# RWKV recurrence: v centred as it is turned, roots written for 64 channels, the crossed block from the masked products, the bonus as two products of a split r k

## The chip, the cores and the metric

The kernel runs on 1 core of one Trainium2 chip. The metric is the device time of one execution in microseconds (us). Three runs of the kernel before gave 2329.27 to 2331.78, with a median of 2330.76.

## The reference, cut to what matters

A two-layer network over 512 tokens of 1024 channels: FFN, an attention mixer, FFN, then a mixer of RWKV-7 heads and chunked attention, an MLP, a convolution and an MLP. The change lies in the RWKV part (8 heads of 64 channels):

```python
    a = jax.nn.sigmoid(a0 + xa @ a2)
    g = jax.nn.sigmoid(xg) @ g2
    kk = heads(k * k_k)
    kk = kk / jnp.maximum(jnp.sqrt(jnp.sum(kk * kk, axis=-1, keepdims=True)), 1e-12)
    k = k * (1 + (a - 1) * k_a)
    y = rwkv7_scan(rh, heads(decay), kh, vh, kk, ah)   # S = S*w - (S kk)(kk a)^T + v k^T ; y = S r
    mean = jnp.mean(y, axis=-1, keepdims=True)
    var = jnp.mean(jnp.square(y - mean), axis=-1, keepdims=True)
    y = (y - mean) * lax.rsqrt(var + GN_EPS)
    y = y * lnx_w + lnx_b
    bonus = jnp.sum(rh * kh * r_k, axis=-1, keepdims=True) * vh
    y = (y + bonus) * g
```

The channel of y is the channel of v, and y is linear in v. So a v whose mean over the head's 64 channels is taken off gives y less its mean.

## The kernel before

All large products are "split": a weight unit (128 rows by 8 blocks of 128, 512 KB) is loaded by SP, its high part is made by ACT (`stream_high`, L101) and its low part by POOL (`stream_low`, L114), and the tensor engine (PE) runs three fp32r products of 512 columns for each block (`split_products`, L133 to L135: high x high, high weight x low, low weight x high). Four slots hold units in a ring. A unit's products may start once its low part is there (`c.s_lo`).

The recurrence works on 4 pairs of heads (`PAIRS`), each pair on all 128 partitions (64 channels a head) and 8 chunks of 64 tokens. For pair j, PE runs `prod` (L1998), `lab` (L2005, and the crossed products L2008), four `turn`s by transposes (L2019: V, B, K, A), five levels of `w` (L2029), `d` (L2049), `e` (L2053), which invert the chunk's triangular matrix, with `lv` (L2036) in level 0, then `u`, `z` (L2060, L2064), `ru`, `g` (L2072, L2076), `yl`, `h` (L2082 to L2090), seven sequential steps `s2` to `s7` (L2100) and `y` (L2115).

The order on each engine is written out by hand, and PE runs its queue in order. Between the steps of pair j stand:

- `fill(j, slot)`: products of pair j+2's input weights, in single blocks (the table `FILL`), so that PE has work while DVE or ACT finish what the next step needs. For pair 3 these belong to the attention that follows.
- `prepare(j+1, part)`: the next pair's inputs. PE: `lora_w`, `lora_a`, `kknorm` (squares summed for a head into 2 columns), `kkb` (L1818: the reciprocal norm spread over 64 channels by `by_channel_pe`), `bonus` (L1939). ACT: shifts k, r, v; `sq`; `root`; `sigw`, `siga`, `ld`, `rks`; the exponentials. DVE: `raw`, `rec`, `L` (a scan), `kk`, `bon`. POOL: `k`, `kk0`, `r`, `v`, `ka`, `kfin`, `rk`, `lp`, `le`, three low parts, then `A`, `b0`, `B`, `K`, `Bp`, `Kp`, `pend`, `R` (L2400 to L2410).
- `tail(j-1, name)`: the previous pair's normalisation. `mean` (L1950: head sums of y, one fp32 product of 512 columns), `yc` (DVE, L2561: y less the mean), `ysq` (ACT), `var` (L1956), `yroot` (ACT), `yrec` (DVE), `yrb` (L1818: spread over channels), `yn`, `ysum` (DVE), `gate` (L1965), `out`.

Each engine counts its steps with a semaphore per list (`PREPARATION`, `STEPS`, `TAIL`); `PL(j, "R")` means "wait for POOL's step R of pair j", `PA`, `PV`, `PE_` the same for ACT, DVE and PE, `TA`, `TV`, `TE` for tails, `V`, `A`, `E` for the steps. Pair 0's preparation runs ahead of the loop, and there `prepare(0, "bonus")` stands on PE right before pair 0's `prod`:

```python
    prepare(0, "kkb")
    unit_part(1, KU + 4, 3 * KU)
    prepare(0, "bonus")
    for j in range(PAIRS):
        q, t = j + 1, j - 1
        if j == 0:
            PL(j, "K")
```

In the loop, `tail(t, "gate")` and `prepare(q, "bonus")` stand behind `h`, ahead of `s2`. On PE `unit_part` waits at a unit's first block for its low part; the second unit of a pair's fill begins at slot 7, behind level 4's `e`.

Of the kernel before, what the change touches and what calls it, by code (L numbers as in the profile page):

```python
# [2169 lines left out]
def rwkv_act(act, c, w, base, m, a, passes):  # L2170
# [15 lines left out]
    def prepare(j, part):  # L2186
# [23 lines left out]
        elif part == "root":  # L2210
            PE_(j, "kknorm")
            prepared("root", act.activation(w.norm[:, 0], ps[:, b_norm, 0:2 * TT].rearrange("p (b s) -> p b s", s=2),
                                            ACT.Sqrt))
# [9 lines left out]
        else:  # L2223
# [9 lines left out]
            prepared("ePe", act.activation(w.ePe, w.ePe, ACT.Exp))  # L2233

    def tail(t, name):
        if t < 0:
            return
        if name == "ysq":
            TV(t, "yc")
            ended("ysq", act.activation(w.ysq, w.yc, ACT.Square))  # L2240
        else:
            TE(t, "var")
            norms = ps[:, tail_banks(base, t)[2], 8:8 + 2 * TT]
            ended("yroot", act.activation(w.ynorm[:, 0], norms.rearrange("p (b s) -> p b s", s=2), ACT.Sqrt,
                                          bias=c.gn_eps[:, 0:1], scale=1.0 / HD))
# [1389 lines left out]
```

## Time and profile before

| | |
|---|---|
| median of three runs | 2330.76 us |
| the profiled execution | 2329.62 us, its span 2327.9 us |
| mean granted clock of PE | 0.993 |
| PE, DVE, ACT, POOL busy | 2289.9 (98%), 1156.0 (50%), 914.2 (39%), 1163.3 (50%) |
| prod of pairs 0 to 3 starts at | 1145.21, 1193.98, 1246.81, 1299.59 us |

Times in rows are from the span's start. A timeline row has the start, the time from the start of the first of its instructions to the end of the last, engine, line, operation, what is written from what, and the count; in brackets is the idle time of the engine before it and what ended it. PE's products overlap: the price of a step is from its start to the start of the next. An fp32 product of 512 columns shows as two records, a transposed block of 128 columns as one.

### The profile page before, as it was taken

The numbers are of one execution on the slowest core, as the hardware profiler recorded it, in microseconds if no ns is written. First come the engines' busy times: TensorE is split into PE (matmuls) and PEld (weight loads), VectorE is DVE, ScalarE is ACT, GpSimd is POOL, SyncE is SP. The second block draws the span as 40 slices with busy tenths as digits, with TensorE's granted clock in tenths as the row PEclk, the third lists the DMA queues.
The fourth block names the chain that finished last, engine by engine and source line by source line (L and its number), as shares of the span: only waits on it lengthen the run. The fifth ranks groups of instructions, "written<-read, shape, count | busy, mean of one in ns | idle before, by whom it ended". The sixth has DMA issues, their size and how long they took to land.

```text
span 2327.9 us, 37006 instructions
## 1 busy us (share of the span) xinstructions
PE 2289.9 (98%) x13984; PEld 1892.3 (81%) x13984; DVE 1156.0 (50%) x1772; ACT 914.2 (39%) x1456; POOL 1163.3 (50%) x687
## 2 busy tenths in 40 slices
PE   8999999999999999999999999999999999999998
PEld 7888887888888888878777778888888878888887
DVE  5442146267744331367554466614626986731732
ACT  5332225467753321255654264222234435222222
POOL 5444444545565554444555444444445973544442
PEclk9999999999999999999999999999999989999999
DMA  4332333320033333331101113332332332333331
GB/s 167 99 97 93 99 99 103 123 65 2 1 101 99 99 99 92 97 126 57 54 30 41 59 51 100 99 99 91 99 99 75 99 100 82 99 99 93 96 97 57
DMA packets 56127, 200.11 MB, mean 86 GB/s; under 512 B 6224, under 2 KB 6480, under 8 KB 56016
## 3 DMA queue, kind: packets, MB, share of 16 engines
q1 hardware_dynamic: 54432, 195.82, 26.5%
q10 hardware_dynamic: 1584, 2.75, 0.4%
q8 instruction: 77, 1.26, 0.2%
q14 instruction: 34, 0.28, 0.0%
HBM read 196.45 MB, written 2.10 MB: 85 GB/s over the span
## 4 chain that ended last, share of the span: by engine, by line
PE 50%; DVE 2%; ACT 1%; POOL 1%; issue 0%; DVEq 0%; ACTq 0%
PE ps L133 15%; PE ps L134 15%; PE ps L135 14%; PE ps L642 1%; DVE ps L3096 0%; PE ps L2053 0%; PE ps L657 0%; POOL sb_w_lo L114 0%; PE ps L2049 0%; PE ps L2100 0%; PE ps L2029 0%; PE ps L1998 0%; PE ps L2019 0%; DVE sb_ak_lo L1015 0%; DVE sb_L L2544 0%
## 5 line engine op out<-in xcount | busy, mean ns | idle before, releaser
L114 POOL TENSOR_TENSOR sb_w_lo<-sb_w_raw,sb_w_hi 128x1024 fp32r<-128x1024 f32 (+1 forms) x361 | 886.2, 2458 | 931.5 <-ACT sb_w_hi L101 930.0
L133 PE MATMUL ps<-sb_xn_hi,sb_w_hi 128*128 128x512 f32 x1688 | 670.3, 397 | 5.9 <-DVE sb_xn_lo L175 3.1
L134 PE MATMUL ps<-sb_xn_lo,sb_w_hi 128*128 128x512 f32 x1688 | 658.4, 390 | 0.0
L135 PE MATMUL ps<-sb_xn_hi,sb_w_lo 128*128 128x512 f32 x1688 | 658.2, 390 | 0.0
L101 ACT ACTIVATE sb_w_hi<-sb_w_raw 128x1024 fp32r<-128x1024 f32 x362 | 379.7, 1055 | 483.8 <-PE ps L135 457.6
L133 PEld LDWEIGHTS ps<-sb_xn_hi,sb_w_hi 128*128 128x128 f32 x1688 | 316.8, 188 | 78.3 <-issue 4.0
L135 PEld LDWEIGHTS ps<-sb_xn_hi,sb_w_lo 128*128 128x128 f32 x1688 | 317.0, 188 | 67.7
L134 PEld LDWEIGHTS ps<-sb_xn_lo,sb_w_hi 128*128 128x128 f32 x1688 | 317.1, 188 | 65.6 <-issue 2.2
L133 PE MATMUL ps<-sb_hid_hi,sb_w_hi 128*128 128x512 f32 x864 | 336.3, 389 | 2.0 <-DVE sb_hid_lo L401 2.0
L135 PE MATMUL ps<-sb_hid_hi,sb_w_lo 128*128 128x512 f32 x864 | 336.1, 389 | 0.0
L134 PE MATMUL ps<-sb_hid_lo,sb_w_hi 128*128 128x512 f32 x864 | 336.1, 389 | 0.0
L133 PEld LDWEIGHTS ps<-sb_hid_hi,sb_w_hi 128*128 128x128 f32 x864 | 162.2, 188 | 36.5 <-DVE sb_hid_lo L401 2.8
L135 PEld LDWEIGHTS ps<-sb_hid_hi,sb_w_lo 128*128 128x128 f32 x864 | 162.2, 188 | 33.8
L134 PEld LDWEIGHTS ps<-sb_hid_lo,sb_w_hi 128*128 128x128 f32 x864 | 162.2, 188 | 33.4
L470 DVE SCALAR_TENSOR_TENSOR ps<-ps,sb_rs 128x512 f32<-128x512 f32 x32 | 22.4, 700 | 286.7 <-PE ps L135 286.7
L2808 DVE TENSOR_TENSOR sb_hid_lo<-sb_h,sb_hid_hi 128x512 f32 x64 | 143.6, 2243 | 7.9
L2792 ACT ACTIVATE sb_gate<-ps 128x512 f32<-128x512 f32 x64 | 38.3, 598 | 248.6 <-PE ps L135 248.6
L393 DVE TENSOR_TENSOR sb_h<-sb_gate,ps 128x512 f32<-128x512 f32 x44 | 30.3, 689 | 207.8 <-PE ps L135 206.2
L401 DVE TENSOR_TENSOR sb_hid_lo<-sb_h,sb_hid_hi 128x512 f32 x44 | 115.8, 2632 | 5.4
L378 ACT ACTIVATE sb_gate<-ps 128x512 f32<-128x512 f32 x44 | 26.4, 600 | 199.6 <-DVE ps L389 199.6
L448 ACT ACTIVATE ps<-ps 128x512 f32<-128x512 f32 x56 | 32.8, 585 | 168.3 <-DVE ps L505 127.6
L502 DVE SCALAR_TENSOR_TENSOR ps<-ps,sb_rs 128x512 f32<-128x512 f32 x32 | 22.4, 700 | 130.5 <-PE ps L135 130.5
(487 smaller groups left out, 2987.4 us busy)
## 6 DMA issues: line engine op xcount, KB each, us to landing
sb_w_raw<-weights SPq DMA_DIRECT2D x365, 512.0 KB, 3.5
sb_stage<-x SPq DMA_DIRECT2D x4, 512.0 KB, 4.8
out<-sb_out_stage SPq DMA_DIRECT2D x8, 256.0 KB, 2.9
sb_abias<-table ACTq DMA_DIRECT2D x4, 256.0 KB, 4.8
sb_lora_w<-lora ACTq DMA_DIRECT2D x2, 256.0 KB, 2.8
sb_rstd<-table ACTq DMA_DIRECT2D x1, 256.0 KB, 2.7
sb_root<-table ACTq DMA_DIRECT2D x1, 256.0 KB, 3.0
sb_ss<-table ACTq DMA_DIRECT2D x1, 256.0 KB, 4.3
```

What stands on the lines that cost most here:

```text
L101: act.activation(c.w_hi[:, slot, 0:width], c.w_raw[:, slot, 0:width], ACT.Copy).then_inc(c.s_hi, 1)
L114: pool.tensor_tensor(c.w_lo[:, slot, 0:width], c.w_raw[:, slot, 0:width], c.w_hi[:, slot, 0:width].bitcast(F32), ALU.subtract).then_inc(c. ...
L133: pe.matmul(out, hi, rhs_hi(k0 + k), start=first, stop=False)
L134: pe.matmul(out, hi, rhs_lo(k0 + k), start=False, stop=False)
L135: mm = pe.matmul(out, lo, rhs_hi(k0 + k), start=False, stop=last)
L378: act.activation(c.gate[:, s // 2], c.ps[:, slot], ACT.Silu).then_inc(c.s_act, 1)
L393: dve.tensor_tensor(c.h[:, f], c.gate[:, f], c.ps[:, u % RING], ALU.mult).then_inc(c.s_evac, 2)
L401: dve.tensor_tensor(c.hid_lo[:, i * 2 + f], c.h[:, f], c.hid_hi[:, i * 2 + f].bitcast(F32), ALU.subtract).then_inc(c.s_hid, 1)
L448: act.activation(c.ps[:, 4 + n % 2], new, ACT.Square).then_inc(c.s_sq, 1)
L642: mm = pe.matmul(c.ps[0:p.kind.rows, T_BANK + bank, col + (i - q0) * P:col + (i - q0) * P + P], a.p[n % 3][:, at:at + p.kind.rows], a.diag ...
L2792: act.activation(c.gate[:, s % 2], c.ps[:, slot], ACT.Relu).then_inc(c.s_act, 1)
L2808: dve.tensor_tensor(c.hid_lo[:, i * RING + s], c.h[:, s % 2], c.hid_hi[:, i * RING + s].bitcast(F32), ALU.subtract).then_inc(c.s_hid, 1)
```

## The change

1. The turn of V becomes an fp32 product with `c.centre` (the identity less 1/64 within a head), so tok's v, and with it y, has no mean over a head. `mean` on PE and `yc` on DVE go; `ysq` reads YL and moves ahead of the turns on ACT, `var` from level 1 to level 0, `yrec` to level 1, and `lora_a` no longer waits for `yc`.
2. The reciprocal is taken first on DVE (`kmax`, `rec`; `yadd`, `yrec`), then ACT takes the root of it, written out over 64 channels (512 columns), and PE spreads it by four plain transposes instead of eight fp32 products (`kkb`, `yrb`).
3. The crossed block E[1] comes from M's second half by two DVE operations of 64 partitions; its 8 products in `lab` go.
4. Of the three weights of a pair, two are split on POOL between `v` and `ka` and on ACT between `value` and `root`; the third stays where it was.
5. `bonus` is two fp32r products of a constant with `rk_hi` (ACT, behind the exponentials) and `rk_lo` (POOL, `rkl` behind `Kp`).

```diff
-    pool = ["k", "kk0", "r", "v", "ka", "kfin", "rk", "lp", "le", "A", "b0", "B", "K", "Bp", "Kp", "pend", "R"]
+    pool = ["k", "kk0", "r", "v", "ka", "kfin", "rk", "lp", "le", "A", "b0", "B", "K", "Bp", "Kp", "rkl", "pend", "R"]
...
-def by_channel_pe(pe, c, bank, norm):
-
-    for b in range(TT):
-        for s in range(2):
-            mm = pe.matmul(c.ps[HALF[s], bank, b * P:b * P + P], norm[:, 1, b, s:s + 1].broadcast_to([P, HD]), c.ident[:],
-                           start=True, stop=True)
-    return mm
+def spread(norm):
+    return norm[:, 1].rearrange("p b s -> p (b s)").unsqueeze(2).broadcast_to([P, 2 * TT, HD])
...
         elif part == "lora_a":
-            if j >= 2:
-                TV(j - 2, "yc")
             mm = pe.matmul(ps[:, b_turned], w.lora_w[HD:P, 0, cols], w.lora_in[HD:P, 0], start=True, stop=True)
         elif part == "kkb":
-            PV(j, "rec")
+            PA(j, "root")
             if j >= 2:
-                TA(j - 2, "yroot")
-            mm = by_channel_pe(pe, c, b_norm, w.norm)
+                TV(j - 2, "yrec")
+            for b in range(TT):
+                mm = pe.transpose(ps[:, b_norm, b * P:b * P + P], w.tmp2[:, b * P:b * P + P], c.ident[:])
         else:
-            PL(j, "rk")
             PV(j, "kk")
-            mm = pe.matmul(ps[:, bonus_bank(u, j)], c.ones_head[:], w.rk, start=True, stop=True)
+            bank = ps[:, bonus_bank(u, j)]
+            PA(j, "rkh")
+            pe.matmul(bank, c.ones_part, w.rk_hi[:], start=True, stop=False)
+            PL(j, "rkl")
+            mm = pe.matmul(bank, c.ones_part, w.rk_lo[:], start=False, stop=True)
...
-        if name == "mean":
-            if t < PAIRS - 1:
+        if name == "var":
+            if t == PAIRS - 2:
                 pe.wait_ge(c.s_evac, first_unit(t + 2) + START + 3)
-            mm = pe.matmul(ps[:, bank], c.ones_head[:], w.YL[:], start=True, stop=True)
-        elif name == "var":
-            if t < PAIRS - 2:
-                PA(t + 2, "root")
             TA(t, "ysq")
...
-            TV(t, "yrec")
-            mm = by_channel_pe(pe, c, bank, w.ynorm)
+            TA(t, "yroot")
+            for b in range(TT):
+                mm = pe.transpose(ps[:, bank, b * P:b * P + P], w.ysq[:, b], c.ident[:])
...
         done("prod", mm)
-        tail(t, "mean")
         fill(j, 0)
...
-        for b, p in ((b, p) for b in range(TT) for p in range(2)):
-            mm = pe.matmul(ps[across(1, p), 5, TT * CH + b * CH:TT * CH + b * CH + CH], w.BK[HALF[1], 2 * b + p, 0],
-                           AR[HALF[1], 0, token(b, p)], start=True, stop=True)
...
-                mm = pe.transpose(ps[:, bank, b * P:b * P + P], sources[x][:, b * P:b * P + P], c.ident[:])
+                turned = ps[:, bank, b * P:b * P + P]
+                if name == "V":
+                    mm = pe.matmul(turned, w.v[:, b * P:b * P + P], c.centre, start=True, stop=True)
+                else:
+                    mm = pe.transpose(turned, sources[x][:, b * P:b * P + P], c.ident[:])
...
             fill(j, 2 + lv)
-            if lv == 1:
+            if lv == 0:
                 tail(t, "var")
...
-    V(t, "y")
-    tail(t, "mean")
     out_early(4, 6)
...
         elif part == "root":
-            PE_(j, "kknorm")
-            prepared("root", act.activation(w.norm[:, 0], ps[:, b_norm, 0:2 * TT].rearrange("p (b s) -> p b s", s=2),
-                                            ACT.Sqrt))
+            PV(j, "rec")
+            prepared("root", act.activation(w.tmp2.rearrange("p (x n) -> p x n", n=HD), spread(w.norm), ACT.Sqrt))
...
+            PL(j, "rk")
+            if j >= 1:
+                PE_(j - 1, "bonus")
+            prepared("rkh", act.activation(w.rk_hi[:], w.rk, ACT.Copy))
...
         if name == "ysq":
-            TV(t, "yc")
-            ended("ysq", act.activation(w.ysq, w.yc, ACT.Square))
+            V(t, "y")
+            ended("ysq", act.activation(w.RU[:], w.YL[:], ACT.Square))
...
+        tail(j - 1, "ysq")
         for name, x, bank in TURNS:
...
-        tail(j - 1, "ysq")
         prepare(j + 1, "value")
+        if j < PAIRS - 1:
+            for u in range(base + 6 + 3 * j, base + 8 + 3 * j):
+                high(u)
...
         if j < PAIRS - 1:
-            for u in range(base + 6 + 3 * j, base + 9 + 3 * j):
-                high(u)
+            high(base + 8 + 3 * j)
...
         shifted(j, 2, "v", w.v)
+        if j >= 1:
+            stream_low(pool, c, base + 6 + 3 * j, base + 8 + 3 * j)
         PA(j, "siga")
...
         if j >= 1:
-            stream_low(pool, c, base + 6 + 3 * j, base + 9 + 3 * j)
+            stream_low(pool, c, base + 8 + 3 * j, base + 9 + 3 * j)
...
         prepared("Kp", pool.tensor_tensor(w.BKp[:, 1], w.k[:], w.ePe, ALU.mult))
+        PA(j, "rkh")
+        prepared("rkl", pool.tensor_tensor(w.rk_lo[:], w.rk, w.rk_hi[:].bitcast(F32), ALU.subtract))
...
-            ended("yc", dve.scalar_tensor_tensor(out=w.yc, in0=blocks(ps[:, bank]), scalar=-1.0 / HD, in1=blocks(w.YL[:]),
-                                                 op0=ALU.mult, op1=ALU.add))
...
+            sums = ps[:, norms, 8:8 + 2 * TT].rearrange("p (b s) -> p b s", s=2)
+            ended("yadd", dve.tensor_scalar(w.ynorm[:, 0], sums, 1.0 / HD, GN_EPS, ALU.mult, ALU.add))
+            ours(t, "yadd")
...
+        own(j, "mm1")
+        dve.tensor_tensor(w.E[HALF[1], 1], w.M[HALF[0], 1, :, 0], first[HALF[0]], ALU.mult)
+        done("em1", dve.tensor_tensor(w.E[HALF[0], 1], w.M[HALF[1], 1, :, 0], first[HALF[1]], ALU.mult))
         E(j, "lab")
-        done("em1", dve.tensor_tensor(w.E[:, 1], ps[:, 5, TT * CH:].rearrange("p (b n) -> p b n", n=CH), first, ALU.mult))
...
-            elif lv == 2:
+            elif lv == 1:
                 prepare(q, "rec")
+                tail(t, "yrec")
...
+        pool.tensor_scalar(c.centre, c.ones_head[:], -1.0 / HD, None, ALU.mult).then_inc(c.s_zeroed, 1)
...
+        pool.tensor_tensor(c.centre, c.centre, c.ident[:], ALU.add).then_inc(c.s_zeroed, 1)
...
+        pool.tensor_tensor(c.ones_part, c.ones_head[:], c.ones_head[:], ALU.mult).then_inc(c.s_zeroed, 1)
```

## Rows read from the trace of the kernel before

**Rows 1.** The page's first part, and the waits of 1145 to 1352 us.

```profile
PE 2289.9 (98%) x13984; PEld 1892.3 (81%) x13984; DVE 1156.0 (50%) x1772; ACT 914.2 (39%) x1456; POOL 1163.3 (50%) x687
...
PE ps L133 <- POOL sb_w_lo L114: 2.9, 3, 1.1
```

**Rows 2.** PE's timeline, pair 1 from prod to level 0.

```profile
1193.98 1.98 PE L1998 MATMUL ps<-sb_AR,sb_BK 64*64 64x128 f32 x64
1195.89 1.12 PE L1950 MATMUL ps<-sb_rYL,sb_ones_head 128*128 128x512 f32 x2
...
1198.33 0.69 PE L2005 MATMUL ps<-sb_BK,sb_AR 64*64 64x64 f32 x32
1198.86 0.63 PE L2008 MATMUL ps<-sb_AR,sb_BK 64*64 64x64 f32 x16
1199.42 0.50 PE L133 MATMUL ps<-sb_xn_hi,sb_w_hi 128*128 128x512 f32 x1
...
1200.22 0.60 PE L2019 MATMUL ps<-sb_ident,sb_rkv 128*128 128x128 f32 x4
...
1202.06 0.69 PE L1921 MATMUL ps<-sb_lora_in,sb_lora_w 64*128 64x512 f32 x1
...
1203.61 0.58 PE L2029 MATMUL ps<-sb_D,sb_M 64*64 64x64 f32 x24
```

**Rows 3.** The same timeline, at kkb and at the bonus of pair 1.

```profile
1216.13 1.09 PE L1818 MATMUL ps<-sb_ident,sb_rwkv_norm 128*64 128x128 f32 x16
1217.16 0.50 PE L133 MATMUL ps<-sb_xn_hi,sb_w_hi 128*128 128x512 f32 x1
...
1232.95 1.02 PE L1939 MATMUL ps<-sb_y,sb_ones_head 128*128 128x512 f32 x2
1233.90 0.33 PE L2100 MATMUL ps<-sb_dist,sb_rG 64*64 64x64 f32 x4
```

**Rows 4.** DVE's timeline, levels 2 and 3 of pair 1.

```profile
1214.77 0.69 DVE L2657 TENSOR_TENSOR sb_D<-sb_D,ps 128x512 f32<-128x512 f32 x1 [0.51 <-PE ps L2049]
...
1216.88 1.75 DVE L2544 TENSOR_TENSOR_SCAN sb_L<-sb_dist_local,sb_ss 128x512 f32<-128x512 bf16 x1
```

**Rows 5.** ACT's timeline in pair 1, behind v2.

```profile
1208.48 1.28 ACT L2212 ACT_TABLE_LOAD   x1
...
1212.67 0.69 ACT L2216 ACTIVATE sb_ss<-ps,sb_par 128x512 f32<-128x512 f32 x1
...
1214.96 2.95 ACT L101 ACTIVATE sb_w_hi<-sb_w_raw 128x1024 fp32r<-128x1024 f32 x3
```

**Rows 6.** POOL's timeline in pair 1, from ka to pend.

```profile
1214.04 0.77 POOL L2385 TENSOR_SCALAR sb_y<-sb_root,sb_par,sb_omka 128x512 f32<-128x512 f32 x1 [4.42 <-ACT sb_root L2218]
...
1218.70 1.27 POOL L2393 TENSOR_TENSOR sb_raw<-sb_L,sb_ss 128x512 f32<-128x512 f32 x1 [1.16 <-DVE sb_L L2544]
...
1220.94 7.00 POOL L114 TENSOR_TENSOR sb_w_lo<-sb_w_raw,sb_w_hi 128x1024 fp32r<-128x1024 f32 x3
1227.89 1.09 POOL L2400 TENSOR_TENSOR sb_AR<-sb_rstd,sb_raw 128x512 f32<-128x512 f32 x1
...
1235.28 0.19 POOL L2407 COPY sb_pend<-sb_eP 128x8 f32<-128x8 f32 x1
```

**Rows 7.** PE's timeline, the last record of pair 0's s2.

```profile
1181.13 0.27 PE L2100 MATMUL ps<-sb_dist,sb_rG 64*64 64x64 f32 x1 [0.54 <-issue]
```

**Rows 8.** Ahead of pair 0: POOL's kfin and pend, PE's first prod.

```profile
1131.90 2.08 POOL L2387 TENSOR_TENSOR sb_rkk<-sb_rkk,sb_y 128x512 f32<-128x512 f32 x1
...
1146.83 0.19 POOL L2407 COPY sb_pend<-sb_eP 128x8 f32<-128x8 f32 x1
...
1145.21 1.98 PE L1998 MATMUL ps<-sb_AR,sb_BK 64*64 64x128 f32 x64
```

**Rows 9.** PE behind its longest idle of this stage; the windows view (busy us by engine, PEclk).

```profile
1068.25 0.39 PE L628 MATMUL ps<-sb_ak_hi,sb_aq 128*128 128x256 f32 x1 [3.09 <-DVE sb_aq L1011]
...
1070.00:1072.00 2.00, 1.27 (x5) 0.86 (x5) 1.97 (x8) 1.51 (x3) 1.90 (x1) 0.50 0.00 0
```

More of the change, by code:

```diff
@@ L1600, in rwkv_preparation @@
     pe = ["lora_w", "lora_a", "kknorm", "kkb", "bonus"]
-    act = ["k1", "k2", "r1", "r2", "sq", "v1", "v2", "root", "sigw", "siga", "ld", "rks", "eP", "ePi", "ePp", "ePn", "ePe"]
-    dve = ["raw1", "raw0", "raw2", "rootmax", "rec", "L", "kk", "bon"]
-    pool = ["k", "kk0", "r", "v", "ka", "kfin", "rk", "lp", "le", "A", "b0", "B", "K", "Bp", "Kp", "pend", "R"]
+    act = ["k1", "k2", "r1", "r2", "sq", "v1", "v2", "root", "sigw", "siga", "ld", "rks", "eP", "ePi", "ePp", "ePn", "ePe", "rkh"]
+    dve = ["raw1", "raw0", "raw2", "kmax", "rec", "L", "kk", "bon"]
+    pool = ["k", "kk0", "r", "v", "ka", "kfin", "rk", "lp", "le", "A", "b0", "B", "K", "Bp", "Kp", "rkl", "pend", "R"]
     return pe, act, dve, pool
@@ L1623, in rwkv_tail @@
 def rwkv_tail():
-    return ["mean", "var", "yrb", "gate"], ["ysq", "yroot"], ["yc", "yrec", "yn", "ysum", "out"]
+    return ["var", "yrb", "gate"], ["ysq", "yroot"], ["yadd", "yrec", "yn", "ysum", "out"]
 PREPARATION = dict(zip(("pe", "act", "dve", "pool"), rwkv_preparation()))
@@ L2238, in tail @@
         if name == "ysq":
-            TV(t, "yc")
-            ended("ysq", act.activation(w.ysq, w.yc, ACT.Square))
-        else:
[L2242 to L2245, printed above, removed]
+            V(t, "y")
+            ended("ysq", act.activation(w.RU[:], w.YL[:], ACT.Square))
+        else:
+            TV(t, "yrec")
+            ended("yroot", act.activation(w.RU[:].rearrange("p (x n) -> p x n", n=HD), spread(w.ynorm), ACT.Sqrt))
     act.wait_ge(c.s_pe, base + START + 1)
@@ L2537, in prepare @@
         elif part == "rec":
-            PA(j, "root")
-            prepared("rootmax", dve.tensor_scalar(w.norm[:, 0], w.norm[:, 0], 1e-12, None, ALU.max))
-            mine(j, "rootmax")
+            PE_(j, "kknorm")
+            sums = ps[:, b_norm, 0:2 * TT].rearrange("p (b s) -> p b s", s=2)
+            prepared("kmax", dve.tensor_scalar(w.norm[:, 0], sums, 1e-24, None, ALU.max))
+            mine(j, "kmax")
             prepared("rec", dve.reciprocal(w.norm[:, 1], w.norm[:, 0]))
@@ L2556, in tail @@
             return
-        bank, b_gate, _ = tail_banks(base, t)
-        if name == "yc":
-            TE(t, "mean")
-            own(t, "y")
-            ended("yc", dve.scalar_tensor_tensor(out=w.yc, in0=blocks(ps[:, bank]), scalar=-1.0 / HD, in1=blocks(w.YL[:]),
-                                                 op0=ALU.mult, op1=ALU.add))
-        elif name == "yrec":
-            TA(t, "yroot")
+        bank, b_gate, norms = tail_banks(base, t)
+        if name == "yrec":
+            TE(t, "var")
+            sums = ps[:, norms, 8:8 + 2 * TT].rearrange("p (b s) -> p b s", s=2)
+            ended("yadd", dve.tensor_scalar(w.ynorm[:, 0], sums, 1.0 / HD, GN_EPS, ALU.mult, ALU.add))
+            ours(t, "yadd")
             ended("yrec", dve.reciprocal(w.ynorm[:, 1], w.ynorm[:, 0]))
@@ L2567, in tail @@
             TE(t, "yrb")
-            ended("yn", dve.scalar_tensor_tensor(out=w.yc, in0=w.yc, scalar=c.column("l0_lnx_w_2", t),
+            ended("yn", dve.scalar_tensor_tensor(out=w.yc, in0=blocks(w.YL[:]), scalar=c.column("l0_lnx_w_2", t),
                                                  in1=blocks(ps[:, bank]), op0=ALU.mult, op1=ALU.mult))
@@ L2637, in rwkv_dve @@
         done("E", dve.tensor_tensor(Et, Et, over(c.ident_head[:]), ALU.add))
-        tail(t, "yc")
         for lv in range(len(LEVELS)):
@@ L2660, in rwkv_dve @@
             done(f"E{lv}", dve.tensor_tensor(Et, Et, banked(4), ALU.add))
-        tail(t, "yrec")
         tail(t, "yn")
@@ L2694, in rwkv_dve @@
     add_early(0)
-    tail(t, "yc")
     maxima(0)
```

8 lines of the change are left out of this document (added).

## The prediction

> **What bounds the kernel.** I read the page first: the matmul engine (PE) is busy for 98% of the span [rows 1], so only PE's time counts, and another engine counts where PE waits for it. The change lies in the recurrence, about 1107 to 1370 us. The chain of waits there shows one wait of weight: PE for a weight's low part from POOL, 2.9 us in three times [rows 1], once in each of pairs 0 to 2, behind level 4. Then I took PE's timeline by start times, since its durations overlap. A slot of one weight row (three fp32r products of 512 columns) takes 0.80 from start to start [rows 2], 0.23 a product. Pairs 1 and 2 last 52.8 us each, nearly all issue. So the first reading is that less PE work is less time; the second, that PE runs its queue in order, and a wait put in it stops everything behind.
>
> **PE work, per pair.** All prices are starts to next starts.
> - "mean" goes: 512 columns in fp32 are two records, 0.95 as in the bonus (below). But prod ends at 1195.89 and lab at the earliest waits for DVE's first mask. The six fill products take 1.6, the mask is ready about 1.4 after prod's end, so lab can start at 1197.5 where it started at 1198.33 [rows 2]. I take 0.85.
> - The crossed products of lab (16 records) go: 0.56 [rows 2], less 0.1 for the change of tile shape that the rest now pays: 0.47.
> - V turned by a product instead of transposes: the 16 transposes of all four turns take 1.84 [rows 2], 0.46 a turn. No fp32 product of 128 by 128 columns stands in this stage; the bounds are two records for each transpose's one (0.9) and kkb's 16 records (1.03). I take 0.95, what as many columns cost in one 512-column product, so +0.5.
> - lora_a in pairs 1 and 2 waited for "yc": the two lora products took 1.55 [rows 2] where with no wait two 64-row halves run side by side in 1.06 (pair 0, 1152.96 to 1154.02). 0.5 gained.
> - kkb and yrb: 16 records, 1.03 [rows 3], against four transposes, 0.44: 0.58 each. Behind kkb stands the scan of L, 1.75 on DVE [rows 4]: D3 is asked for 0.4 before the scan ends, so of kkb's 0.58 I count 0.2.
> - The wait for the low weight goes: 2.9 idle, and by start times 0.7, 1.2 and 1.2. Next late there is E4 on DVE, which comes about 0.1 before u: covered, barely.
> - var moves one level up, at the same cost; the roots' 0.24 wait ahead of it goes. The reciprocals with their maximum and sum now all stand between W1 and D1 on DVE; ahead of D2, with two of them in place, it still idled 0.51 [rows 4], the price of the two more is 0.4. If they came later, D1 and w2 would, by as much. The second half of E costs DVE 0.35 more (256 columns, half of a 0.69 operation); PE has the turns and loras above it, except in pair 0, where w0 stands right behind E: +0.35 there.
>
> In pair 1: 0.85 + 0.47 - 0.5 + 0.5 + 0.24 + 0.2 + 1.2 + 0.58 = 3.5, so PE reaches the bonus at 1229.4 instead of 1232.95 [rows 3].
>
> **The bonus** is two fp32r products at 0.23, about 0.65 with the changes of shape, 0.3 less than the one in fp32. But its second product waits for rkl, which POOL makes behind A, b0, B, K, Bp, Kp. This is the step that decides, so I follow the chain.
> - ACT, pair 1: v2 ended at 1208.46 (the table load follows at 1208.48); ysq moves ahead (0.5 less), PE's earlier lv takes 1.3 off: 1206.7. Two high parts at 0.98, table load 1.28, both roots now 512 wide at 0.62 (as ACT's other 512-column operations), table load 1.28, sigw 0.59, siga 0.68 [rows 5]: 7.03, so siga ends at 1213.7; before, ka started at 1214.04.
> - POOL: its two low parts now lie in the idle stretch before siga, done by 1212.6. ka, kfin, rk to 1217.3 (3.5), lp and le 2.24, one low part 2.33, A to Kp 7.39 (1227.89 to 1235.28), rkl 1.25 as its like lp [rows 6]. Sum: 1213.8 + 3.5 + 2.24 + 2.33 + 7.39 + 1.25 = 1230.5.
> PE wants it at 1229.6, behind the first product, and waits 0.9. s2 then starts at 1230.9 instead of 1233.90: 3.0 gained in each of pairs 1 and 2.
> - Pair 0: in pair 1 rkl comes 36.5 after prod's start. In pair 0 ACT has no yroot (0.6 less), but lv comes 0.9 later, since DVE makes bon and three raws before the mask, and b0 ran 0.4 shorter: 36.4. PE's bonus stood 33.9 after prod (1179.07); less 0.7 and 0.2, plus 0.35, it would be there at 33.3 and, behind the first product, waits 2.8. The four records of s2 are then through at 37.0; before, the last one started at 1181.13, 35.9 after prod, behind an issue gap of 0.54 that a wait hides [rows 7]: +1.0.
> - Before pair 0: POOL's Kp ends at 1146.83; the longer root adds 0.44, rkl 1.25: 1148.5. PE comes to the bonus at 1143.7 (kkb 0.58 earlier), runs one product, and waits 4.5 us with prod behind, which before only needed K. Prod starts at 1148.9 instead of 1145.21 [rows 8]: +3.7. Nothing covers this; DVE's bon and the next pair's raw come later by as much.
> - Pair 3: mean 0.85, lab 0.47, yrb 0.58, less 0.5 for V and 0.1 for tA: 1.3 gained. The last tail: mean 0.95 and yrb 0.58, of which softmax waits give part back: 1.0 (0 to 1.5).
> Three constants on POOL, the rkh on ACT (0.6, before u is asked for) and the weights high earlier: nothing, POOL and ACT idle there; without that cover rkh would cost 0.6 a pair.
>
> Sum: 3.7 + 1.0 - 3.0 - 3.0 - 1.3 - 1.0 = -3.6 us.
>
> **The clock.** PE idled 3.1 us before 1068.25, and the granted clock fell from 2.4 to 1.2 GHz (0.50 in the stretch after) [rows 9]; products of 512 columns then started 0.43 apart instead of 0.23. Here 4.5 us idle are made ahead of pair 0. I take the fall as happening: bonus and prod are 2.4 slower, the fill loses 0.3, and lab's slack of 0.5 takes some: +2.2 (bounds: 0 with no fall; 3.2 if all work up to lab runs at half speed and no slack helps). Pair 0's wait of 2.8 us at the bonus is just under the one seen; I count no fall there. The Trainium skill (TensorE: Matmul & The Clock Gate, Part 1) says that the throttled clock is the default and that activity releases it, so that an idle gap costs more than its own length. By that rule this change, whose gains are less PE work, gives part of them back, and without it the sum would stay at -3.6; the trace agrees with the rule in the one gap shown.
>
> Result: -3.6 + 2.2 = -1.4. The profiled execution took 2329.62, so 2328.2; the median, 1.14 above it, 2330.76, so **2329.4 us**: no change. A measurement tells about 0.2% here, 4.7 us.
>
> **Rivals.**
> - *PE's work alone decides* (rkl is ready in time, because POOL's chain is shorter than I make it). Then the prelude gives 1.0, pair 0 0.55, pairs 1 and 2 3.9 each, pair 3 1.3, tail 1.0: -11.7, so 2319.1. For it: POOL is idle half the time, and my chain adds ten durations. Against: the order of the queue, which the prelude shows in absolute times. If the chain is only 1.5 us shorter everywhere, the waits ahead of pair 0 and in it give 3.0, those of pairs 1 and 2 1.8, and with the clock's fall -1.4 becomes -6.2: 2324.6. Chance 0.25 for both together.
> - *POOL's chain is longer, and PE's clock falls twice* (slower). Place: from siga to rkl. POOL's kfin took 2.08 in the prelude beside DVE [rows 8], and 1.28 elsewhere (lp 1.27 [rows 6]); two such of ten operations make a pair's chain 1.5 longer. Then three pairs lose 4.5, and pair 0's wait is past 4 us, so the clock falls there too, +2.6: -1.4 + 4.5 + 2.6 = +5.7, 2336.5. It decides from 1.2 us a pair up. The Trainium skill (SBUF, two separate sides) has a rule for it: a DVE operation with two SBUF inputs and a GpSimd operation exclude each other on a shared port pair; the halves of E and the roots' move make a few more of these. The trace has both durations, so it does not speak against it. Chance 0.23.
> - *No fall of the clock*: 2327.2. Chance 0.12.
> - The forecast itself, 0.40.
>
> **Numbers.** Faster by over 0.2% (below 2326.1) 0.25, within 0.2% 0.52, slower 0.23. The range reaches from the shorter chain, less 1.6 for the prices of V, the tail and E, to the slower rival: 2323 to 2337.
>
> **What would show it.** PE: a gap of over 4 us between two products of the bonus ahead of the first prod, ended by POOL; gaps near 3, 1 and 1 us at the same line in pairs 0 to 2; no wait for the low weight behind level 4; clock 0.5 after the first gap. From prod to prod about 49.8 us in pairs 1 and 2 (52.8 before); in pair 0 49.8 (48.8 before), or 52 with the clock's fall. Four records each for kkb and yrb. POOL: two low parts between v and ka. It is wrong if the gap ahead of prod is under 3 us, or if pairs 1 and 2 shrink by less than 2.

## The result: slower by 0.4%

The kernel after takes **2339.93 us** (median of 6 runs, 2337.16 to 2342.99), the kernel before beside it 2330.60 (6 runs, 2329.27 to 2335.48). The ratio is 1.0039 with a 95% interval of 1.0028 to 1.0050. The prediction was 2329.4 in a range of 2323 to 2337 with "no change" as the likeliest: the time lies outside, on the slow side. The profiled execution of the kernel after took 2341.02 us with a span of 2339.3, 11.4 more than the 2327.9 of before. The medians are 9.3 apart: what follows splits up the 11.4 of the two traces.

The page of the kernel after, and its waits between 1140 and 1360 us, against [rows 1]:

```profile
PE 2288.0 (98%) x13832; PEld 1892.9 (81%) x13832; DVE 1157.0 (49%) x1776; ACT 919.8 (39%) x1460; POOL 1175.0 (50%) x694
...
PE ps L1937 <- POOL sb_rk_lo L2406: 13.4, 4, 5.6
```

PE has 152 instructions and 1.9 us of work less, and the wait for the low weight is gone. In its place stands a larger one: the second product of the bonus waits four times for POOL's low part of r k, 13.4 us in all. A gap below is the time from the start of PE's last product to the start of the next one; the bracket in a row is the idle time, which is shorter. The four gaps are 5.97, 3.63, 3.13 and 3.14 us. Here are the first and the third in PE's timeline:

```profile
1143.22 0.40 PE L1935 MATMUL ps<-sb_rk_hi,sb_ones_part 128*128 128x512 f32 x1
1149.19 0.79 PE L1937 MATMUL ps<-sb_rk_lo,sb_ones_part 128*128 128x512 f32 x1 [5.57 <-POOL sb_rk_lo L2406]
1149.92 3.62 PE L1993 MATMUL ps<-sb_AR,sb_BK 64*64 64x128 f32 x64
...
1238.18 0.79 PE L1935 MATMUL ps<-sb_rk_hi,sb_ones_part 128*128 128x512 f32 x1
1241.31 0.51 PE L1937 MATMUL ps<-sb_rk_lo,sb_ones_part 128*128 128x512 f32 x1 [2.34 <-POOL sb_rk_lo L2406]
1241.75 0.33 PE L2095 MATMUL ps<-sb_dist,sb_rG 64*64 64x64 f32 x4
```

In or behind each of them the granted clock falls, and once more in the last tail. The windows view of the kernel after (stretch, length, busy us of PE, PEld, DVE, ACT, POOL, then PEclk, DMA share, GB/s) shows 0.50 to 0.52, 1.2 GHz, behind the first, third and fourth, and in the tail:

```profile
1150.00:1152.00 2.00, 2.00 (x40) 2.00 (x44) 1.98 (x4) 0.59 (x1) 0.00 (x0) 0.50 0.04 8
...
1242.00:1244.00 2.00, 2.00 (x12) 1.13 (x8) 0.22 (x1) 0.00 (x0) 0.62 (x1) 0.52 0.00 0
...
1296.00:1298.00 2.00, 2.00 (x8) 1.12 (x7) 0.22 (x1) 0.00 (x0) 1.34 (x1) 0.50 0.00 0
...
1372.00:1374.00 2.00, 2.00 (x9) 1.90 (x8) 0.48 (x3) 1.66 (x5) 0.26 (x1) 0.50 0.00 0
```

The 64 records of prod take 3.62 in the first fence; at full clock they took 1.98 [rows 2]. From the first product of each pair to that of the next (for pair 3: to y), in us:

| | prod of pair 0 | pair 0 | pair 1 | pair 2 | pair 3 | y to last gate |
|---|---|---|---|---|---|---|
| before | 1145.21 | 48.77 | 52.83 | 52.78 | 49.37 | 11.60 |
| after | 1149.92 | 53.91 | 52.30 | 53.52 | 47.99 | 12.78 |
| after less before | +4.7 | +5.1 | -0.5 | +0.7 | -1.4 | +1.2 |

The columns add up to +9.9 at the last gate. Another 1.5 come in the 6 us behind it, where the clock falls once more; at 1375.70 the kernel after is 11.4 behind the kernel before, and the spans end 11.4 apart. That last place is one that I had not looked for. PE is done with the fill ahead of pair 3's gate at about 1367.2 and starts the gate at 1370.42. The rows of POOL, DVE and ACT there:

```profile
1362.54 2.38 POOL L114 TENSOR_TENSOR sb_w_lo<-sb_w_raw,sb_w_hi 128x1024 fp32r<-128x1024 f32 x1
...
1362.76 2.19 DVE L766 TENSOR_SCALAR sb_t_negmax<-sb_t_maxima 128x4 f32<-128x4 f32 x1
...
1365.29 0.63 ACT L2239 ACTIVATE sb_rRU<-sb_rwkv_ynorm 128x512 f32<-128x512 f32 x1 [2.50 <-DVE sb_rwkv_ynorm L2564]
1365.94 1.28 ACT L705 ACT_TABLE_LOAD   x1
...
1369.56 0.18 DVE L778 RECIPROCAL sb_t_scale<-sb_t_sums 128x4 f32<-128x4 f32 x1 [1.90 <-ACT sb_later_p L705]
1369.65 0.72 DVE L2567 SCALAR_TENSOR_TENSOR sb_rH<-sb_rYL,sb_par,ps 128x512 f32<-128x512 f32 x1
```

Read it upwards: the gate waits for yn (L2567), which stands on DVE behind scale(0) (L778), which waits for softmax(0) on ACT (it starts with the table load), which stands behind yroot (L2239), which waits for yrec on DVE, behind maxima(0). The last step of maxima(0), L766 on 128 by 4 numbers, took 2.19 us; the same line took 0.17 in the next pass (1367.49). In the kernel before it took 0.63, and yroot did not wait for it:

```profile
1355.62 0.63 DVE L766 TENSOR_SCALAR sb_t_negmax<-sb_t_maxima 128x4 f32<-128x4 f32 x1
...
1355.76 0.27 ACT L2244 ACTIVATE sb_rwkv_ynorm<-ps,sb_gn_eps 128x8 f32<-128x8 f32 x1
1356.05 1.28 ACT L705 ACT_TABLE_LOAD   x1
```

The table load starts 7.1 us behind y there and 8.3 behind it in the kernel after (1348.96 to 1356.05, 1357.64 to 1365.94).

### The profile page after: what moved, and what is told of

Its sections match the earlier page's. It is cut to its first block, busy times and chain, and to the rows that moved or that the text cites. A ratio compares the mean times of both kernels' runs of the same rounds, so it can differ in the third digit from the quotient of the medians.

```text
span 2339.3 us, 36715 instructions
## 1 busy us (share of the span) xinstructions
PE 2288.0 (98%) x13832; PEld 1892.9 (81%) x13832; DVE 1157.0 (49%) x1776; ACT 919.8 (39%) x1460; POOL 1175.0 (50%) x694
## 3 DMA queue, kind: packets, MB, share of 16 engines
q10 hardware_dynamic: 1584, 2.75, 0.3%
q8 instruction: 75, 1.23, 0.2%
## 4 chain that ended last, share of the span: by engine, by line
PE 41%; POOL 7%; issue 3%; DVE 2%; ACT 2%; POOLq 0%; DVEq 0%; ACTq 0%
PE ps L133 12%; PE ps L134 12%; PE ps L135 12%; POOL sb_w_lo L114 2%; POOL sb_caway L3052 1%; PE ps L642 1%; DVE ps L3103 0%; PE ps L1993 0%; PE ps L657 0%; POOL sb_cu_lo L3064 0%; POOL sb_y L2388 0%; ACT sb_w_hi L101 0%; POOL sb_cout L3058 0%; PE ps L2095 0%; POOL sb_rkk L2385 0%
## 5 line engine op out<-in xcount | busy, mean ns | idle before, releaser
L2815 DVE TENSOR_TENSOR sb_hid_lo<-sb_h,sb_hid_hi 128x512 f32 x64 | 151.5, 2367 | 7.9
L401 DVE TENSOR_TENSOR sb_hid_lo<-sb_h,sb_hid_hi 128x512 f32 x44 | 115.8, 2633 | 5.4
```

The costliest lines, as they stand in the source:

```text
L401: dve.tensor_tensor(c.hid_lo[:, i * 2 + f], c.h[:, f], c.hid_hi[:, i * 2 + f].bitcast(F32), ALU.subtract).then_inc(c.s_hid, 1)
L2815: dve.tensor_tensor(c.hid_lo[:, i * RING + s], c.h[:, s % 2], c.hid_hi[:, i * RING + s].bitcast(F32), ALU.subtract).then_inc(c.s_hid, 1)
```

## The experiments

Waits below are gaps from start to start; a time is a median, a ratio is against the kernel before run beside it. Starts, gaps and lengths of pairs are from the one profiled execution of each kernel, which can be up to 3.9 us from the median.

### One product again

```diff
+            PL(j, "rk")
...
-            PA(j, "rkh")
-            pe.matmul(bank, c.ones_part, w.rk_hi[:], start=True, stop=False)
-            PL(j, "rkl")
-            mm = pe.matmul(bank, c.ones_part, w.rk_lo[:], start=False, stop=True)
+            mm = pe.matmul(ps[:, bonus_bank(u, j)], c.ones_head[:], w.rk, start=True, stop=True)
```

> The kernel after with the split of the bonus alone undone: one fp32 product of ones_head and r k again, no high part on ACT, no low part on POOL; everything else stays. Theory A (the second product's wait for POOL's low part, and the clock that falls behind it, are the loss): the four gaps of 5.97, 3.63, 3.13 and 3.14 us are gone, the first product of pair 0 starts near 1145.5 (K's end) in place of 1149.9, and the granted clock stays at 1.00 from 1140 to 1360 but for the last tail; prelude -4.4, pair 0 -5, pairs 1 and 2 -4 to -5 each: 2321 to 2326 us. Theory B (the added work of TensorE is the loss: V as fp32 product, two products, more waits behind them): at most the gaps go and come back at the next wait, 2334 or more. Theory C (POOL's chain A to Kp, later by contention, is the loss): only the prelude changes, 2335 to 2337.

Measured: 2323.98 us, ratio 0.9971 (0.9960 to 0.9982); prod of pair 0 at 1145.60, pairs of 48.78, 49.43, 49.42 and 47.95. Theory A holds and its number with it: 16 us under the kernel after, and 0.3% faster than before. What is left of the loss is in the last tail, whose gap of 3.49 and clock of 0.50 are still there.

### The split kept, its low part early

```diff
+        PA(j, "rkh")
+        prepared("rkl", pool.tensor_tensor(w.rk_lo[:], w.rk, w.rk_hi[:].bitcast(F32), ALU.subtract))
         if j >= 1:
             stream_low(pool, c, base + 8 + 3 * j, base + 9 + 3 * j)
         PV(j, "kk")
...
-        PA(j, "rkh")
-        prepared("rkl", pool.tensor_tensor(w.rk_lo[:], w.rk, w.rk_hi[:].bitcast(F32), ALU.subtract))
```

On ACT the high part stands between ePi and ePp.

> The kernel after with the split kept and only moved: ACT makes the high part behind ePi, POOL the low part right behind le and ahead of A. Theory A: the second product waits for nothing in pairs 0 to 2; in the prelude A to K stand about 0.6 to 1.3 us later, so the first product of pair 0 starts at 1146.0 to 1146.8; pairs 0, 1, 2 shrink as without the split and by some 0.2 each more, since the two products take 0.65 and one takes 0.95: 2321 to 2327 us, within 1.5 us of the kernel with one product. Theory B: 2334 or more. Theory C: POOL's chain is longer in every pair (its operations take 2.1 in place of 1.3 us wherever they stand), a new wait takes the place of the old one: 2332 to 2337.

Measured: 2324.30 us, ratio 0.9973 (0.9963 to 0.9983); prod of pair 0 at 1146.30, pairs of 48.77, 49.17, 49.17 and 47.98. Same operations, same engines, another place in POOL's queue, and 15.6 us less. PE at pair 1's bonus, first with one product, then with two:

```profile
1229.95 1.02 PE L1934 MATMUL ps<-sb_y,sb_ones_head 128*128 128x512 f32 x2
1230.90 0.33 PE L2092 MATMUL ps<-sb_dist,sb_rG 64*64 64x64 f32 x4
```

```profile
1229.78 1.13 PE L1960 MATMUL ps<-sb_lora_in,sb_lora_w 128*128 128x512 f32 x2
1230.34 0.80 PE L1935 MATMUL ps<-sb_rk_hi,sb_ones_part 128*128 128x512 f32 x1
1230.97 0.40 PE L1937 MATMUL ps<-sb_rk_lo,sb_ones_part 128*128 128x512 f32 x1
1231.33 0.33 PE L2095 MATMUL ps<-sb_dist,sb_rG 64*64 64x64 f32 x4
```

The two products take 0.99 from start to start and the one takes 0.95. The saving of 0.26 in pairs 1 and 2 (49.43 to 49.17) comes from the gate in front: its two records take 0.56 where they took 0.96 ahead of the fp32 product, and 0.1 of that is lost on the way to the gate. Pair 0 saves nothing. With POOL's low part ahead of A, K is ready 0.7 later for pair 0, which gives all of the 0.5 back. Free of its wait, the split is worth nothing that can be measured.

### Only TensorE's order changed

```diff
                 fill(j, 8 + ch)
+                if ch == 5:
+                    prepared("bonus", bonus_low(q))
```

`bonus_low` is the wait for rkl and the second product, taken out of the bonus of pairs 1 to 3.

> The kernel after with TensorE's order alone changed: in pairs 0 to 2 the second product of the bonus of the next pair stands behind the fill of the fifth chunk's step, four fills later, in place of right behind the first product. POOL and ACT are untouched, and the prelude keeps its wait of 6 us and its low clock. Theory A: no wait in pairs 0 to 2 and no low clock there; pair 0 keeps 1.6 for the clock it inherits from the prelude: 50.4, pairs 1 and 2 49.1 to 49.3 us long: 2327 to 2329.5 us. Rival (TensorE's wait only moves: DVE's bon or the next pair's products find POOL late): pairs 1 and 2 over 51, 2334 or more.

Measured: 2328.64 us, ratio 0.9989 (0.9980 to 0.9998); pairs of 50.00, 49.49, 49.51 and 47.97. POOL is as late as in the kernel after (rkl ends 37.4 behind prod in both); four fills of 0.9 us now stand between the two products, and PE does not wait at the second. The time is inside theory A's range; pairs 1 and 2 are 0.2 above it and pair 0 is 0.4 under. The prelude's gap of 5.97 is still there. So the loss in pairs 0 to 2 was the place at which PE asked, not POOL's work.

### The low part one operation earlier

```diff
         prepared("Bp", pool.tensor_tensor(w.BKp[:, 0], w.tmp, w.ePe, ALU.mult))
+        PA(j, "rkh")
+        prepared("rkl", pool.tensor_tensor(w.rk_lo[:], w.rk, w.rk_hi[:].bitcast(F32), ALU.subtract))
         prepared("Kp", pool.tensor_tensor(w.BKp[:, 1], w.k[:], w.ePe, ALU.mult))
-        PA(j, "rkh")
-        prepared("rkl", pool.tensor_tensor(w.rk_lo[:], w.rk, w.rk_hi[:].bitcast(F32), ALU.subtract))
```

> The kernel after with POOL's low part one operation (1.26 us) earlier, behind Bp and ahead of Kp. The waits are then 4.7 in the prelude, 2.4 in pair 0, 1.9 in pairs 1 and 2 by every theory. If the low clock is what such a wait brings whatever its length, the gain is the waits' own, 4 times 1.26: 2334.5 to 2335.5 us, and the granted clock still falls to 0.50 in each pair. If the clock's fall hangs on the length of the wait, it stays at 1.00 in pairs 1 and 2, perhaps in pair 0, and 1.5 to 1.7 more go with each: 2329.5 to 2332.5.

Measured: 2332.11 us, ratio 1.0005 (0.9995 to 1.0016; one of the 11 executions took 5033.68, the others 2330.09 to 2338.51), 7.8 under the kernel after where the four waits are only 1.23, 1.22, 1.22 and 1.23 shorter. The gaps are 4.74, 2.41, 1.91 and 1.91 us. The windows of this kernel behind the second and third:

```profile
1190.00:1192.00 2.00, 2.00 (x9) 1.13 (x8) 0.22 (x1) 0.00 (x0) 0.00 (x0) 0.50 0.00 0
...
1242.00:1244.00 2.00, 2.00 (x14) 1.29 (x14) 1.04 (x3) 0.00 (x0) 0.00 (x0) 1.00 0.00 0
```

Pair 0 (54.07) still has the fall, pairs 1 and 2 have not, and they are 49.55 and 49.59 long, against 52.30 and 53.52. So a wait shortened by 1.2 gave 2.75 and 3.93: the rest, 1.5 and 2.7, is what the clock took in those two traces. The time is inside the range of a fall that hangs on the wait's length; that length alone does not decide it, as the counts further down show.

### The split alone, on the kernel before

```diff
-            mm = pe.matmul(ps[:, bonus_bank(u, j)], c.ones_head[:], w.rk, start=True, stop=True)
...
+            pe.matmul(bank, c.ones_part, w.rk_hi[:], start=True, stop=False)
+            PL(j, "rkl")
+            mm = pe.matmul(bank, c.ones_part, w.rk_lo[:], start=False, stop=True)
```

> The kernel before with the split of the bonus alone (two products, high part behind ePe on ACT, low part behind Kp on POOL). Theory A: the second product waits 4 to 5 us in the prelude and 2 to 3.5 in pairs 0 to 2, with clock falls behind most of them: +4 in the prelude, +2 to +5 in each of the three pairs: 2341 to 2349 us. Theory B: the split costs what its products and waits of work cost, under 0.5 a pair, and the prelude's 4: 2335 at most. Theory C (POOL is late only because of the weight parts moved ahead of the gates): waits of under 2 in pairs 1 and 2 and no clock fall there, 2336 to 2339.

Measured: 2355.34 us, ratio 1.0108 (1.0093 to 1.0124), above even theory A's range. The gaps are 3.88, 5.71, 4.03 and 4.14, the pairs 56.42, 58.81, 60.21 and 49.35 long. I had the waits of pairs 0 to 2 at 2 to 3.5 and a loss of 2 to 5 in each. In pair 1 a gap of 4.03 came with 6.0 us of loss; the windows show a low clock for most of 6 us behind it:

```profile
1250.00:1252.00 2.00, 2.00 (x8) 1.13 (x8) 0.23 (x3) 0.00 (x0) 0.00 (x0) 0.50 0.00 0
1252.00:1254.00 2.00, 2.00 (x8) 1.14 (x8) 0.83 (x3) 0.00 (x0) 0.00 (x0) 0.50 0.00 0
1254.00:1256.00 2.00, 2.00 (x9) 1.14 (x9) 0.33 (x2) 0.00 (x0) 0.00 (x0) 0.65 0.00 0
```

PE ran 8 records in 2 us, where it ran 14 at full clock in the fence of the experiment before this one. Pair 2 lost 7.4. The other parts of the change thus save 15 us beside the split (2355.34 to 2339.93).

### yn ahead of scale(0) in the last tail

```diff
     maxima(1)
+    tail(t, "yn")
     scale(0)
-    tail(t, "yn")
```

> The kernel after with one line of DVE's last tail moved: yn ahead of scale(0). Theory A (the last tail's 2.75 us are TensorE's wait of 3.26 at the gate, for yn behind scale(0) behind softmax(0), and the clock that falls behind it): yn ends near 1368.4 in place of 1370.37, the wait is 1.2 to 1.4, the clock stays at 1.00 there, and the time is 3.0 to 3.6 lower than the kernel after's, 2336.3 to 2336.9. Rival: scale(0) is then 0.7 later and turned attention waits for it: 0 to 1 lower, 2339 to 2340. No other stage changes in either.

Measured: 2336.72 us, ratio 1.0031 (1.0022 to 1.0040): 3.2 under the kernel after, by one line. PE now waits 1.03 at the gate (a gap of 1.43) and the clock stays at 1.00:

```profile
1367.39 1.12 PE L1960 MATMUL ps<-sb_lora_in,sb_lora_w 128*128 128x512 f32 x2 [1.03 <-DVE sb_rH L2567]
```

This kernel also tells how far one trace may be trusted. It is the kernel after up to the last tail, and still its pairs 0 to 2 took 55.29, 52.24 and 50.75 where those of the kernel after took 53.91, 52.30 and 53.52: the clock fell at other times, and in pair 2, behind a gap of 2.24, not at all. What one trace says of the cost of a fall in a pair can be off by 1 to 3 us; the medians are the firmer proof.

### Both moves together

The two edits just shown: rkl behind le, and

```diff
+    tail(t, "yn")
     scale(0)
-    tail(t, "yn")
```

> Both moves together: the low part of r k right behind le, and yn ahead of scale(0) in the last tail. Theory A (the two losses are separate): 3.2 under the kernel with the early low part alone, as the second move gave alone: 2320.5 to 2321.8 us, TensorE's wait at the last gate 1.2 to 1.4 in place of 3.27. Rival: the 3.2 were mostly the clock that fell behind the wait in the kernel after, and with the early low part the clock doesn't fall there: then 2.0 lower at most, 2322.3 or more.

Measured: **2322.22 us**, ratio 0.9962 (0.9949 to 0.9976), 2.1 under the early low part alone. That is between the two expectations and nearer to the rival's: the gap at the gate goes from 3.49 to 1.43 (2.06), and behind the 3.49 of the kernel with the early low part alone the clock had stayed at 1.00 in its trace, so there was nothing more to win there. The two medians are too near to each other (5 executions of 2321.07 to 2322.32, 9 of 2322.97 to 2327.21) to tell 2.1 from 3.2 with certainty.

### The three weights behind the gates again

On top of the early low part, the order of before for a pair's weights:

```diff
-        if j >= 1:
-            stream_low(pool, c, base + 6 + 3 * j, base + 8 + 3 * j)
...
-            stream_low(pool, c, base + 8 + 3 * j, base + 9 + 3 * j)
+            stream_low(pool, c, base + 6 + 3 * j, base + 9 + 3 * j)
```

> The kernel with the early low part of r k, with the three weights of each pair split behind the gates again as before (high parts on ACT behind the gates, low parts on POOL behind le and the low part of r k). Prediction's term: TensorE waits for the third weights' low part again, 0.7 in pair 0 and 1.2 in pairs 1 and 2, 3.1 in all: 2327.0 to 2328.0 us. Rival 1 (that wait is covered by another one ahead of the same step, the scan L and kk on DVE): under 1 more, 2325.3 or less. Rival 2 (POOL's chain behind the weights is 3.7 later, so A to R and the low parts come late for the next pair): over 5 more, 2329.5 or more.

Measured: 2337.88 us, ratio 1.0036 (1.0022 to 1.0050), 13.6 more: my term of 3.1 was too small by a factor of four. The time is in the range of rival 2, but of what that names only the low parts are late: no gap of over 1.25 us waits for A to R, beside the 2.50 ahead of prod which the kernel with the early low part alone has too. Pairs 0 to 2 are 51.65, 55.20 and 54.09 long (48.77, 49.17 and 49.17 with the weights ahead). PE and POOL in pair 1:

```profile
1223.23 0.52 PE L2048 MATMUL ps<-sb_E,sb_W 64*64 64x64 f32 x12
1227.76 0.80 PE L133 MATMUL ps<-sb_xn_hi,sb_w_hi 128*128 128x512 f32 x1 [4.02 <-POOL sb_w_lo L114]
```

```profile
1224.14 1.27 POOL L2391 TENSOR_TENSOR sb_rk_lo<-sb_y,sb_rk_hi 128x512 fp32r<-128x512 f32 x1 [0.37 <-ACT sb_rk_hi L2223]
1225.36 4.66 POOL L114 TENSOR_TENSOR sb_w_lo<-sb_w_raw,sb_w_hi 128x1024 fp32r<-128x1024 f32 x2
```

Against the kernel before, PE asks for this weight 2.2 us earlier in the pair (25.8 behind prod, against 28.0) and POOL has it 0.7 later, behind rkl: a gap of 1.34 becomes 4.24, and the clock falls at 1226.4, inside it. Work taken off PE ahead of a wait only lengthens the wait.

### The same part alone, on the kernel before

```diff
+        if j >= 1:
+            stream_low(pool, c, base + 6 + 3 * j, base + 8 + 3 * j)
         PA(j, "siga")
...
-            stream_low(pool, c, base + 6 + 3 * j, base + 9 + 3 * j)
+            stream_low(pool, c, base + 8 + 3 * j, base + 9 + 3 * j)
```

On ACT two of the three high parts move ahead of root.

> The kernel before with one part of the change alone: two of the three weights of each pair split ahead of the gates. Term of the prediction (TensorE's wait for the first low part, 0.7 in pair 0 and about 1.1 in pairs 1 and 2, goes): 2.4 to 3.0 lower, 2327.1 to 2328.0 us, pairs 1 and 2 51.7 to 51.8 long. Rival (the gates' chain ka to L to kk is late next, since POOL and ACT now reach it behind the weights): under 1 lower, 2329.2 to 2330.6. The 13.6 that undoing this part cost above must then come from the other parts having brought TensorE to that step 2 us earlier.

Measured: 2335.08 us, ratio 1.0020 (1.0011 to 1.0029): 4.0 over the kernel before beside it (2331.07), where I had 2.4 to 3.0 under it. Neither theory named what happens. The old wait is gone, and a new one stands at level 1; PE and ACT in pair 1:

```profile
1207.63 0.40 PE L135 MATMUL ps<-sb_xn_hi,sb_w_lo 128*128 128x512 f32 x1
1210.10 1.77 PE L1956 MATMUL ps<-sb_ones_head,sb_rRU 128*128 128x2 f32 x8 [2.07 <-ACT sb_rwkv_norm L2212]
```

```profile
1206.57 1.99 ACT L101 ACTIVATE sb_w_hi<-sb_w_raw 128x1024 fp32r<-128x1024 f32 x2
1208.58 1.28 ACT L2212 ACT_TABLE_LOAD   x1
1209.87 0.18 ACT L2212 ACTIVATE sb_rwkv_norm<-ps 128x8 f32<-128x8 f32 x1
```

```profile
1212.00:1214.00 2.00, 2.00 (x58) 2.00 (x55) 0.69 (x1) 1.97 (x3) 0.43 (x1) 0.50 0.82 248
```

The wait is only part of the loss. Pairs 1 and 2 are 56.63 and 55.26 long, 3.8 and 2.5 over the kernel before, while PE's waits in each grew by 1.0 (from 1.1 for the weight and 0.4 in small ones to 2.1 for the root and 0.4). The rest goes with the clock, which fell behind both gaps of 2.47 (the last fence has its row in pair 1).

In the kernel before, var waits for the root of the next pair, and the root now stands behind two high parts. The change also takes that wait away (the reciprocal is on DVE, the wait moves to kkb). This part needs the others: alone it costs 4.0, with them it is worth 13.6.

### V turned by transposes

```diff
-                    mm = pe.matmul(turned, w.v[:, b * P:b * P + P], c.centre, start=True, stop=True)
+                    mm = pe.transpose(turned, sources[x][:, b * P:b * P + P], c.ident[:])
```

On top of both moves; it leaves out the centring of v.

> The kernel with both moves, with V turned by transposes again in place of the product with the centring matrix; this leaves out the centring of v, and so the mean of y is not taken out. Term of the prediction (V as product 0.5 a pair, all of it on TensorE's path): 4 times 0.43 lower, 2320.2 to 2321.0 us, each pair 48.7 in place of 49.1. Rival (the turns stand beside a wait for dm on DVE, or ACT's copies bound the next step, so the product costs nothing): 2321.7 to 2322.7.

Measured: 2321.90 us, ratio 0.9962 (0.9948 to 0.9975); pairs of 48.73, 49.11, 49.17 and 47.51, against 48.79, 49.11, 49.15 and 47.98. The rival holds in pairs 0 to 2, the term only in pair 3 (0.47):

```profile
1199.71 0.60 PE L2011 MATMUL ps<-sb_ident,sb_rkv 128*128 128x128 f32 x4
1200.14 0.60 PE L2011 MATMUL ps<-sb_ident,sb_BKp 128*128 128x128 f32 x4
1201.15 0.66 PE L2011 MATMUL ps<-sb_ident,sb_BKp 128*128 128x128 f32 x4 [0.41 <-DVE sb_D L2631]
```

The faster turn of V runs into a wait for DVE's step `dm`, which makes D from the products of lab. The turns take 2.47 in both kernels (1199.71 to 1202.18 here, 1199.21 to 1201.68 with the product).

### One product and yn first

```diff
+            mm = pe.matmul(ps[:, bonus_bank(u, j)], c.ones_head[:], w.rk, start=True, stop=True)
...
+    tail(t, "yn")
     scale(0)
-    tail(t, "yn")
```

> The kernel after with one fp32 product for the bonus and with yn ahead of scale(0). If the split is worth nothing once it waits for nothing (pairs 0.26 longer with one product, its first product of pair 0 0.7 earlier): 2320.6 to 2322.3 us, within 1 us of the kernel with both moves (2322.2). If the split is worth the 0.3 a pair that the pairs show, or more: 2322.5 to 2324. The wait at the last gate is 1.2 and the clock stays at 1.00 behind it.

Measured: 2321.27 us, ratio 0.9960 (0.9946 to 0.9973), within 1 us of the split with both moves. The two versions are equal, and both beat the kernel before by 0.4%.

## Why the prediction was wrong

The mechanism was the one that I named as the step that decides; its size was wrong, and one place was not seen. By the steps:

- **PE's prices held.** By start times of pair 1, prod to lab is 3.51 (4.35 before: 0.84, I had 0.85), lab 0.62 (1.09: 0.47 as said), the loras 1.07 (0.5 as said), kkb 0.41 and yrb 0.53 (0.44 each), the wait for the low weight is gone in all three pairs. V as a product takes 0.89 (I had 0.95), and the run with V turned by transposes shows it to be covered by dm in pairs 0 to 2.
- **The wait for rkl in pairs 1 and 2** was put at 0.9 and is 2.9 (a gap of 3.13 less 0.23 for the first product). Half of the error is on PE's side: it is at the bonus 34.35 behind prod, where I had 35.4. The missed 1.1 is the gate's 0.40 and 0.6 in the products of yl and h. Half is on POOL's: ka starts 19.84 behind prod, as worked out (19.8), but rkl ends 37.4 behind it instead of 36.5. Its rk and B are longer, and both overlap an operation of DVE (for rk the scan of L):

```profile
1225.15 1.76 DVE L2545 TENSOR_TENSOR_SCAN sb_L<-sb_dist_local,sb_ss 128x512 f32<-128x512 bf16 x1
...
1225.90 2.08 POOL L2388 TENSOR_TENSOR sb_y<-sb_y,sb_rkk 128x512 f32<-128x512 f32 x1
...
1234.94 1.59 POOL L2401 TENSOR_TENSOR sb_BK<-sb_y,sb_raw 128x512 f32<-128x512 f32 x1
```

  In the kernel before, rk began ahead of the scan (1216.88 [rows 4]) and took 1.28:

```profile
1216.26 1.28 POOL L2390 TENSOR_TENSOR sb_y<-sb_y,sb_rkk 128x512 f32<-128x512 f32 x1
```

  I had rk at 1.28 and B at 1.09; b0 was 0.4 shorter, so the chain is 0.9 longer in all. That the overlap is the cause is read from the rows; no run moved the scan. The slower rival had this (1.5 more a pair), and I gave it 0.23.
- **Pair 0**: a gap of 3.63 instead of 2.8 and the first product, and a fall of the clock that the text counted out ("just under the one seen"): 53.91 instead of 52. **The prelude**: prod at +4.7 instead of +3.7, since lp and le took 1.74 and 2.02 instead of 1.30 and 1.50. The fall's price in pair 0 was put too high: the run with the second product behind the fills, which keeps this fall and waits for POOL nowhere in pair 0, took 50.00 where the kernels without a fall took 48.77, so 1.2 at most, and the second product takes 0.73 where it takes 0.44: at most 1.5 of the 2.2. In the kernel with both moves the clock fell too: prod took 3.31 in place of 1.91 and lab started 0.6 later, and still the pair was no longer for it (48.79).
- **The clock was counted once and fell five times.** The text took the one fall seen, behind 3.1 us, as a border, and all its other waits lay under it. Even with the waits as forecast that was a choice that the trace of before could not bear: it had one such row. In pairs 1 and 2 the falls cost 1.5 and 2.7, by the run with the low part one operation earlier.
- **The last tail** was put at -1.0 and gave +2.7 (+8.7 at y, +11.4 behind the tail). "Of which softmax waits give part back" was all that the text had; the chain from yadd over yroot and softmax(0) to yn was never followed through DVE's order. yadd now stands behind maxima(0), and yroot, and all of softmax(0), behind it. The Trainium skill (SBUF — State Buffer, "SBUF: two separate sides") says that a DVE and a GpSimd operation can exclude each other on a shared port pair for a whole instruction. The trace agrees: L766, on 128 by 4 numbers, took 2.19 and ended at 1364.95, 0.03 behind POOL's low part beside it. It took 2.17 in the kernel with both moves, and in the kernel before, where it began later beside that low part, 0.63; it ended 0.02 and 0.03 behind the low part there too. No run moved that low part, so this cause is read from the rows and not shown.

Summed by the forecast's own list: prelude +3.7 became +4.7; pair 0, with the clock inherited, +3.2 (1.0 and 2.2) became +5.1; pairs 1 and 2 -6.0 became +0.2; pair 3 -1.3 became -1.4; the tail -1.0 became +2.7. So -1.4 became +11.4 (the rounded terms add up to 11.3). The largest error, 6.2, sits in pairs 1 and 2, and the text's own test (it is wrong "if pairs 1 and 2 shrink by less than 2") names it. The step that failed is the price of the second product's wait there: 0.9 us with no fall of the clock, where the traces show 2.9 and a fall behind each. The rival without the wait was nearly right as a statement on the rest: it gave 2319.1, and without wait and tail the kernel takes 2321 to 2322.

What stays open is when the clock falls. Between 1140 and 1380 us, in the 13 traces together, it did so in or behind every gap of 3.6 us and more (12), 7 of 9 of 3.1 to 3.5, 4 of 9 of 2.2 to 2.9, and none of 1.91 and less. At the gap of 3.4 of [rows 9] it fell in all 13. A gap of 2.50 ahead of prod left the clock at 1.00 with the early low part and took it to 0.50 with both moves, where the same instructions stand there.

## What to carry to other kernels

Splitting an operand for a cheaper product puts two more operations on other engines in front of it: put them where those engines stand idle, or put work of the busy engine between the two products, before counting the saving. Price a wait of the matmul engine at its length plus, where the clock can fall, half-speed work behind it; here 1.2 us less of waiting gave 2.8 to 3.9 in the two pairs where the fall went too. And when work is taken off an engine that runs in order, look at every wait behind it as a wait for a fixed time: it grows by what was saved, and a part of a change tried alone can cost what it is worth beside the others.
